# Gather with the one-hot stationary, expert order by a rank product, 22 instead of 25 units in the last layer

## The chip, the cores and the metric

The kernel runs on one core of a Trainium2 chip. The metric is the time of one execution in device microseconds. Three runs of the kernel before took 2532.23, 2533.88 and 2536.08 us; the median is 2533.88.

## The reference

Two layers of a transformer over 256 context tokens and 256 latent tokens with 1024 channels, all in float32. Each layer has a normalisation and one input projection, four groups of heads (gated delta rule, latent attention, windowed attention, dense attention), an output projection and a residual; the change touches none of that. Then comes a mixture of experts, which is the part that the change is in:

```python
scores = sigmoid(h @ router_w)                      # tokens x 64 experts
_, idx = top_k(scores + router_bias, 6)
gates = take(scores, idx); gates = gates / sum(gates) * 2.5
# for each token: sum over its 6 experts of
#   gate * ((silu(h @ gate_w[e]) * (h @ up_w[e])) @ down_w[e])
routed + swiglu(h, shared_gu, shared_down)
```

Each expert has 1024 x 768 gate and up weights and 384 x 1024 down weights. The first layer routes 512 tokens, the last layer only the 256 latent ones, since only these are the output.

## The kernel before

The mixture of experts is worked in units of 128 rows (slots). A unit takes the tokens of one to four experts, in groups of 32 slots: one expert with all four groups, one with three groups and another with one, two experts with two groups each, or four experts with one group each (a quad). Experts are sorted by how many tokens chose them (`cnt`, `key`, `rank`), and the rank decides the kind of unit. In the last layer there are 25 units: 4 of one expert, 4 of 3 + 1 groups, 8 pairs, 9 quads; `last_work` (L658) puts their order down, a quad, then a unit of one or (3 + 1) kind and a pair, and so on. Two units of the shared expert (n = 0 and 1) come before all of them. `EARLY` is 2, the number of the first routed unit.

Weights come in tiles of [128 x 3072] words (1536 KB), three for each expert: `lo` and `hi` (the lower and upper half of the contraction of gate and up) and `down`. SyncE's queue loads them in the order in which TensorE uses them, lo(n), hi(n), down(n-1), into a ring of nine tiles (`ring`, L721): a load is issued when the part that used the tile before has been multiplied. The loads' experts are read from `eid`; the first layer waits twice for it, for its first eight entries and then (`sorted_ready`, L1021) for all 64. The ninth load waits for that in the first layer.

For each unit n of the last layer, TensorE does in this order (L1769 to L1783): the lo part, the transposes of the activations of n-1 (`act_transposed`), the gate rows of n-1 (`gate_rows`), the hi part, the first pair of combining products of n-2 (`combine`), the gather of n+1 (`gather_by_product`, L1704), the second pair, and the down product of n-1. `gather_by_product` makes the transposed rows of the unit's tokens at once: for each of eight slices of channels and two tiles of tokens it multiplies the tokens (stationary, 128 columns) with a one-hot matrix `hot` of token and slot (128 columns moving), and VectorE copies the result to `hgT` (`unit_copied`, L2601). VectorE also multiplies silu by up (`unit_times`), makes the one-hots (`one_hot`), adds the combined rows (`added`) and copies half of each unit's result (`unit_out`); ScalarE computes silu, copies transposed activations and the other half. The first layer gathers by an indirect DMA of GpSimd and then transposes on TensorE (`unit_transposed`, L1642).

Before the units stands the routing, mostly a chain on VectorE (L2732 to L2817), where each step waits for the one before (`link`): scores plus bias, the eight largest and their indices for each tile of tokens, one-hot over chosen experts, their sum `mask`; TensorE sums the mask to positions and counts (`positions`, L1543); then the sort key, ranks, and in the first layer the lists of tokens by unit. There the order `eid` comes from eight rounds of maximum, index and replacement (`sorted_round`, L2763), the first before the ranks and seven after the lists. In the last layer it comes from a one-hot by rank and a product (`order_of_experts`, L1559).

Of the kernel before, what the change touches and what calls it, by code (L numbers as in the profile page):

```python
# [13 lines left out]
P = 128  # L14
# [23 lines left out]
NT = 4  # L38
# [29 lines left out]
for _n, _w in (("ident", P), ("inc_f", P), ("inc_b", P), ("str_f", P), ("str_b", P), ("ones", P), ("eye64", HALF),  # L68
               ("blocks_f", 3 * HALF), ("blocks_b", 3 * HALF), ("window", 2 * SEQ), ("cos_hd", 2 * 6 * HD),
               ("sin_hd", 2 * 6 * HD), ("cos_pe", 2 * HEADS * MLA_ROPE), ("sin_pe", 2 * HEADS * MLA_ROPE),  # L70
               ("experts", NE), ("slot_no", P), ("codes", NT * CODES)):
# [5 lines left out]
LAST_CAPS = ((4, 4), (4, 3), (16, 2), (40, 1))  # L77


def last_columns():  # L80

    whole = [[(u, i) for i in range(4)] for u in range(4)]
    big = [[(u, 0), (u, 1), (u, 2), (67 - u, 0)] for u in range(4, 8)]
    pair = [[(r, 0), (r, 1), (r + 1, 0), (r + 1, 1)] for r in range(8, 24, 2)]
    quad = [[(r + i, 0) for i in range(4)] for r in range(24, 60, 4)]
    return whole + big + pair + quad
# [10 lines left out]
for _n, _w in (("col_rank", N_COL), ("col_from", N_COL), ("marked", P), ("slot_of", 4), ("index", 1)):  # L97
    TABLE[_n] = (_at, _at + _w)
    _at += _w
# [15 lines left out]
def constants():  # L115
# [30 lines left out]
    put("slot_no", np.arange(P)[None, :])  # L146
    token = np.arange(P)[:, None, None] + P * np.arange(NT)[None, :, None]
# [11 lines left out]
    row("index", p[:, None])  # L159
# [46 lines left out]
def build(nc, x, c, ctx, c_ctx, w_mod, b_mod, norm1_g, norm2_g, rows, taps, w_in, w_up, w_out, router_w,  # L206
          exp_w_gu, exp_w_down, shared_w_gu, shared_w_down, consts, out):
    with ExitStack() as stack:
# [190 lines left out]
        cnt, key, rank, base, cap, left = (scratch(NE) for _ in range(6))  # L399
        gate = sb("gate", [P, NT, 8])  # L400
        beats = carve(stat, 224, NE)
        unit_hot = carve(stat, 288, NE)
        row64 = carve(stat, 352, NE)
# [37 lines left out]
        gated = [carve(htreg, 3072, 2 * P), carve(htreg, 3584, 2 * P)]  # L441
# [192 lines left out]
        order_psum = Order("order_psum", ("router", "pos", "rank", "list"),  # L634
                           ("router", "pos", "marks", "eid", "places", "shares", "rank"))
        order_made = Order("order_made", ("mask", "beats", "listT"), ("mask", "perm", "beats", "shares", "rank"))
# [12 lines left out]
        gate_psum = sig("gate_psum", [N_LAST])  # L649
        gated_ready = sig("gated_ready", [N_LAST])  # L650
# [7 lines left out]
        def last_work():  # L658

            units = {kind: [u for u in range(N_LAST) if KIND_OF[u] == kind] for kind in range(4)}  # L660
            order = []
            for i, quad in enumerate(units[3]):
                order.append(quad)
                if i < 4:
                    order += [units[0][i], units[2][i]]
                elif i < 8:
                    order += [units[1][i - 4], units[2][i]]
# [68 lines left out]
        slotT_psum = sig("slotT_psum", NQ)  # L736
# [350 lines left out]
        def _(pe):  # L1087
# [83 lines left out]
            for l in LAYERS:  # L1171
# [386 lines left out]

                def order_of_experts():  # L1559
# [197 lines left out]
                if l == LAST:  # L1757
# [11 lines left out]
                    for n in range(EARLY, NW[l] + 1):  # L1769
# [11 lines left out]
                        if n >= EARLY + 2:  # L1781
                            combine(n - 2, 1)
# [1286 lines left out]
```

## Time and profile before

| | |
|---|---|
| profiled execution | 2537.54 us, span 2535.7 us, mean granted TensorE clock 0.969 |
| TensorE (PE) busy | 2305.1 us, 91% of the span |
| VectorE (DVE) busy | 792.5 us, 31% |
| ScalarE (ACT) busy | 403.7 us, 16% |
| GpSimd (POOL) busy | 229.0 us, 9% |
| expert loads | 256 + 128 of 1536 KB each, both layers |
| costliest line | L1675 (lo and hi parts), 749.0 us busy, 119.0 us idle before |
| gather by product, L1715 | 191.5 us busy, 800 records |

Line numbers are those of the kernel before. A busy matmul is an occupied one, not one at peak; a share of DMA is the mean of 16 engines. PEld is the load of the stationary operand, which runs beside the products. One float32 product shows as two records.

### The profile page before, as it was taken

How to read it: one execution, taken by the hardware profiler on the slowest of the kernel's cores; microseconds unless marked ns; L12 is line 12 of the kernel's file. 1: busy time of each engine (PE TensorE's matmuls, PEld its weight loads, DVE VectorE, ACT ScalarE, POOL GpSimd, SP SyncE). 2: the span in 40 equal slices, each digit the busy share in tenths (PEclk: the TensorE clock that was granted, in tenths of full speed). 3: DMA queues.
4: the chain of work that ended last, by engine and by line, in shares of the span. 5: the costliest groups of instructions: out<-in, count | busy, mean ns of one | idle time of the engine just before them, and what ended most of it. 6: DMA issues, size and time to landing. Idle time of an engine off the chain costs nothing. (4 is left out here: it accounts for less than half of the span.)

```text
span 2535.7 us, 40724 instructions
## 1 busy us (share of the span) xinstructions
PE 2305.1 (91%) x17170; PEld 1241.6 (49%) x17170; DVE 792.5 (31%) x1709; ACT 403.7 (16%) x860; POOL 229.0 (9%) x286
## 2 busy tenths in 40 slices
PE   6999899999877888888897998899999999999998
PEld 2456744454333343334343556755655565555553
DVE  2375745262110101111112546753222222212123
ACT  2323344110000000000001233352000000000000
POOL 0007200011101111110001005300000000000000
PEclk9999999999999999999998999999999999999999
DMA  8000197359999999999997310015999999999997
GB/s 333 34 17 36 65 379 305 135 226 413 427 426 417 417 419 417 417 419 399 385 422 303 129 50 21 28 47 212 404 390 377 376 423 367 429 412 424 408 416 297
DMA packets 86042, 762.18 MB, mean 301 GB/s; under 512 B 14376, under 2 KB 14904, under 8 KB 27232
## 3 DMA queue, kind: packets, MB, share of 16 engines
q1 hardware_dynamic: 74720, 734.30, 70.3%
q0 software_dynamic: 11136, 25.20, 2.6%
q8 instruction: 141, 2.31, 0.3%
q14 instruction: 45, 0.37, 0.0%
HBM read 748.54 MB, written 23.49 MB: 304 GB/s over the span
## 5 line engine op out<-in xcount | busy, mean ns | idle before, releaser
L1675 PE MATMUL banks<-arena,htreg 128*32 128x384 f32 (+2 forms) x5312 | 749.0, 521 | 119.0 <-DMA arena<-in_exp_w_gu 113.8
L1675 PEld LDWEIGHTS banks<-arena,htreg 128*32 128x32 f32 (+2 forms) x5312 | 331.7, 132 | 527.4 <-issue 435.1
L1700 PE MATMUL banks<-arena,modreg 128*32 128x512 f32 (+2 forms) x1992 | 351.6, 597 | 20.4 <-issue 19.1
L2556 DVE TENSOR_TENSOR modreg<-modreg,banks 128x384 f32<-128x384 f32 x65 | 36.0, 554 | 687.1 <-ACT modreg L2056 687.1
L1700 PEld LDWEIGHTS banks<-arena,modreg 128*32 128x32 f32 (+2 forms) x1992 | 117.4, 126 | 222.1 <-issue 220.7
L1715 PEld LDWEIGHTS banks<-htreg,hreg 128*128 128x128 f32 x800 | 194.2, 334 | 8.7 <-issue 5.9
L1715 PE MATMUL banks<-htreg,hreg 128*128 128x128 f32 x800 | 191.5, 398 | 0.0
L1196 PE MATMUL banks<-arena,htreg 128*128 128x512 f32 (+3 forms) x480 | 158.9, 490 | 0.0
L2079 ACT ACTIVATE modreg<-banks 128x512 f32<-128x512 f32 x58 | 34.7, 598 | 589.5 <-PE banks L1700 589.5
L2617 DVE COPY modreg<-banks 128x512 f32<-128x512 f32 x58 | 40.1, 692 | 268.5 <-PE banks L1700 268.5
L1196 PEld LDWEIGHTS banks<-arena,htreg 128*128 128x128 f32 x480 | 89.6, 191 | 65.0 <-issue 61.0
L1742 PE MATMUL banks<-modreg,htreg 128*128 128x512 f32 x200 | 98.0, 614 | 3.1 <-issue 2.0
L2056 ACT ACTIVATE modreg<-banks 128x384 f32<-128x384 f32 x65 | 31.9, 491 | 432.0 <-PE banks L1675 432.0
L2062 ACT ACTIVATE modreg<-banks 128x384 f32<-128x384 f32 x65 | 31.9, 491 | 422.8 <-PE banks L1691 422.8
L2604 DVE COPY htreg<-banks 128x512 f32<-128x512 f32 x61 | 42.2, 691 | 170.4 <-PE banks L1715 167.6
L1515 PE MATMUL banks<-arena,htreg 128*128 128x512 f32 x192 | 83.2, 593 | 0.0
L2972 POOL DMA_INDIRECT htreg<-h_d,lsg x34 | 35.1, 1032 | 514.5 <-PE banks L1653 472.8
L1184 PE MATMUL banks<-htreg,arena 128*128 128x512 f32 (+1 forms) x192 | 76.1, 558 | 1.2 <-ACTq L780 0.8
L1470 PE MATMUL banks<-arena 64*128 64x512 f32 (+3 forms) x144 | 71.6, 579 | 2.5 <-ACT arena L1990 2.5
L2663 DVE TENSOR_TENSOR hreg<-hreg,banks 128x512 f32<-128x512 f32 x96 | 63.8, 684 | 6.9 <-PE banks L1742 5.9
L1289 PE MATMUL banks<-arena 64*64 64x64 f32 x1280 | 52.8, 224 | 10.7 <-DVE arena L2476 4.0
L1515 PEld LDWEIGHTS banks<-arena,htreg 128*128 128x128 f32 x192 | 36.2, 190 | 44.1 <-issue 44.0
(439 smaller groups left out, 2235.3 us busy)
## 6 DMA issues: line engine op xcount, KB each, us to landing
arena<-in_exp_w_gu SPq DMA_DIRECT2D x256, 1536.0 KB, 17.3
arena<-in_exp_w_down SPq DMA_DIRECT2D x128, 1536.0 KB, 21.5
arena<-in_w_mod SPq DMA_DIRECT2D x32, 1024.0 KB, 9.9
modreg<-in_w_mod SPq DMA_DIRECT2D x14, 1024.0 KB, 8.0
arena<-y_d SPq DMA_DIRECT2D x4, 3072.0 KB, 17.8
modreg<-mod_d SPq DMA_DIRECT2D x20, 512.0 KB
arena<-in_shared_w_gu SPq DMA_DIRECT2D x6, 1536.0 KB
arena<-in_w_in SPq DMA_DIRECT2D x4, 2048.0 KB, 12.7
```

Source lines behind the costliest of these rows:

```text
L1184: last = mm(qkv_bank(ct)[:, lo:], win_qkv[:, k, tok(ct)], hT[:, k, lo:], start=(i == 0), stop=(i == KD - 1))
L1196: last = mm(ps[2 + n % 4][:, lo:w], hT[:, k, tok(t)], win[g][:, k, lo:w], start=(k == 0), stop=(k == KD - 1))
L1289: last = mm(out[r, at + HALF * g:at + HALF * g + HALF], lhs(r, g), rhs(r, g), start=True, stop=True)
L1470: mm(ps[s % 2][:, 0:nk * P], q_, k_, start=True, stop=True).then_inc(scores_psum.sem, 1)
L1515: last = mm(ps[2 + n % 2][:], mixT[:, k, tok(t)], wout[:, k, 512 * half:512 * half + 512], start=(k == 0), stop=(k == KD - 1))
L1675: last = mm(gu_bank(n, half)[rows, 0:DE], src[:, k, rows], up4[q][:, i, DE * half:DE * (half + 1)], start=(k == 0), stop=(k == KD - 1))
L1700: last = mm(ps[4 + half][rows, :], actT[:, k, rows], dn3[q][:, k, 512 * half:512 * half + 512], start=(k == 0), stop=(k == KE - 1))
L1715: last = mm(ps[k // 4][:, tok(k % 4)], rows[:, k, :], hot[r % 2][:, j, :], start=(j == 0), stop=(j == 1))
L1742: mm(comb_bank(n, j, half), gated[r % 2][:, P * j:P * j + P], outs[r % 2][:, 512 * half:512 * half + 512], start=True, stop=True).then_inc ...
L2604: dve.tensor_copy(hgT[q % 2][:, 0:4, :], ps[0][:].rearrange("p (k n) -> p k n", k=4))
L2617: dve.tensor_copy(outs[r % 2][:, 512:1024], ps[5][:]).then_inc(unit_y.sem, 1)
L2663: tt(acc_last[:, j, cols], acc_last[:, j, cols], gu_bank(n + 1, half)[:], ALU.add).then_inc(comb_added.sem, 1)
```

## The change

In the last layer the gather is turned round: the one-hot is stationary and the tokens move, 512 columns at a time, so four products give the unit's rows [128 slots x 1024]. ScalarE copies them to `hrow` in two halves, TensorE transposes them in eight pieces (`rows_transposed`, behind the second pair of combining products), and VectorE copies these to `hgT` as before, now behind both pairs of additions. The capacities change: no unit of one expert is left; 4 units of 3 + 1 groups, 8 pairs and 10 quads make 22, and the order becomes quad, one or two others, quad. In both layers the mask is made by comparing the scores with a copy in which the six largest have been replaced; indices and one-hots come later (first layer: right behind the mask; last layer: behind the first unit's copy). In the first layer the sort rounds 2 to 8 are replaced by a one-hot by rank, a product with the column 0 to 63 (`index`, moved to the other table of constants) and a copy; and the position products move ahead of the lo part of unit 1.

```diff
-LAST_CAPS = ((4, 4), (4, 3), (16, 2), (40, 1))
+LAST_CAPS = ((4, 3), (16, 2), (44, 1))
-    whole = [[(u, i) for i in range(4)] for u in range(4)]
-    big = [[(u, 0), (u, 1), (u, 2), (67 - u, 0)] for u in range(4, 8)]
-    pair = [[(r, 0), (r, 1), (r + 1, 0), (r + 1, 1)] for r in range(8, 24, 2)]
-    quad = [[(r + i, 0) for i in range(4)] for r in range(24, 60, 4)]
+    big = [[(u, 0), (u, 1), (u, 2), (63 - u, 0)] for u in range(4)]
+    pair = [[(r, 0), (r, 1), (r + 1, 0), (r + 1, 1)] for r in range(4, 20, 2)]
+    quad = [[(r + i, 0) for i in range(4)] for r in range(20, 60, 4)]
...
+            others = [u for two in zip(others[4:8] + others[0:2], others[8:12] + others[2:4]) for u in two]
-            for i, quad in enumerate(units[3]):
+            for i, quad in enumerate(quads):
                 order.append(quad)
+                gaps = len(quads) - 1
+                order += others[len(others) * i // gaps:len(others) * (i + 1) // gaps]
...
+                def experts_by_rank():
+                    pe.wait_ge(order_made.sem, order_made.after(l, "perm"))
+                    mm(ps[1][0:1, 384:384 + NE], K("index")[0:NE], by_rank, start=True, stop=True).then_inc(order_psum.sem, 1)
...
+                    for half in range(2):
+                        cols = slice(512 * half, 512 * half + 512)
+                        for j in range(2):
+                            last = mm(ps[half], hot[r % 2][:, j, :], h[:, 2 + j, cols], start=(j == 0), stop=(j == 1))
+                        last.then_inc(slotT_psum.sem, 1)
+                def rows_transposed(n):
+                    r = n - EARLY
+                    pe.wait_ge(slot_rows.sem, slot_rows.at(0, 2 * r + 2))
+                    src = hrow.rearrange("p (d k) -> p k d", k=KD)
                     for k in range(KD):
-                        for j in range(2):
-                            rows = h[:, 2 + j, :].rearrange("p (d k) -> p k d", k=KD)
-                            last = mm(ps[k // 4][:, tok(k % 4)], rows[:, k, :], hot[r % 2][:, j, :], start=(j == 0), stop=(j == 1))
+                        last = pe.transpose(ps[k // 4][:, tok(k % 4)], src[:, k, :], ident)
                     last.then_inc(slotT_psum.sem, 1)
...
                         if n >= EARLY + 2:
                             combine(n - 2, 1)
+                        if n + 1 < NW[l]:
+                            rows_transposed(n + 1)
                         unit_down(n - 1)
...
+                    positions()
                     unit_part(1, "lo")
-                    positions()
                     act_transposed(0)
                     ranks()
+                    experts_by_rank()
...
+                    def slot_rows_copied(n):
+                        r = n - EARLY
+                        for half in range(2):
+                            act.wait_ge(slotT_psum.sem, slotT_psum.at(LAST, 3 * r + half + 1))
+                            fn(hrow[:, 512 * half:512 * half + 512], ps[half][:], ACT.Copy).then_inc(slot_rows.sem, 1)
...
                             added(n - 2, 0)
+                            added(n - 2, 1)
                         if n + 1 < NW[l]:
                             unit_copied(n + 1)
-                        if n >= EARLY + 2:
-                            added(n - 2, 1)
...
-                    link(dve.max_index(out=idx8[:, i, :], in_max=top8[:, i, :], in_values=selb[:, i, :]))
-                link(dve.tensor_copy(idxf[:, nt_, :], idx8[:, nt_, :]))
+                link(dve.tensor_copy(top6[:, nt_, 0:TOPK], top8[:, nt_, 0:TOPK]))
                 for i in range(n_t):
-                    link(tt(onehot[:, i], bc(K("experts"), 1, TOPK), bc(idxf[:, i, 0:TOPK], 2, NE), ALU.is_equal))
-                    ins = red(mask[:, i, :], onehot[:, i].rearrange("p k e -> p e k"), AX, ALU.add)
...
+                    link(dve.match_replace(out=adr[:, i, :], in_to_replace=top6[:, i, :], in_values=selb[:, i, :], imm_value=-3e38))
+                tt(mask[:, nt_, :], selb[:, nt_, :], adr[:, nt_, :], ALU.not_equal).then_inc(order_made.sem, 1)
...
+                ts(by_rank, K("experts")[lo64], rankcol[lo64], None, ALU.is_equal).then_inc(order_made.sem, 1)
...
+                dve.wait_ge(order_psum.sem, order_psum.after(l, "eid"))
+                dve.tensor_copy(eid[0:1, 8:NE], ps[1][0:1, 392:384 + NE]).then_inc(sorted_ready.sem, 1)
...
-                for j in range(1, NE // 8):
-                    sorted_round(j)
```

## Rows read from the trace of the kernel before

**Rows 1.** Stretches of time: stretch, us, busy us (instructions) by engine, clock, DMA share, GB/s.
```profile
1850.00:2140.00 290.00, 290.00 (x1603) 165.15 (x1600) 65.06 (x113) 16.30 (x31) 0.00 (x0) 1.00 0.94 390
2140.00:2450.00 310.00, 300.03 (x2014) 162.51 (x2014) 64.65 (x113) 15.81 (x30) 0.00 (x0) 0.97 1.00 420
2150.00:2200.00 50.00, 50.00 (x341) 25.92 (x338) 10.20 (x18) 3.16 (x6) 0.00 (x0) 1.00 1.01 429
...
556.00:562.00 6.00, 4.91 (x16) 2.32 (x14) 3.08 (x15) 0.60 (x1) 0.30 (x1) 0.90 0.56 165
640.00:1190.00 550.00, 447.41 (x3059) 203.80 (x3052) 59.36 (x95) 36.95 (x70) 67.25 (x67) 0.93 1.01 419
```

**Rows 2.** The same view, two stretches of 10 us in the last layer.
```profile
1920.00:1930.00 10.00, 10.00 (x75) 3.29 (x75) 2.71 (x5) 0.60 (x1) 0.00 (x0) 1.00 0.40 139
...
2220.00:2230.00 10.00, 8.14 (x66) 3.13 (x67) 0.00 (x0) 0.49 (x1) 0.00 (x0) 0.68 1.01 429
```

**Rows 3.** Waits in the last layer: who waited for whom, us, times, longest.
```profile
PE banks L1675 <- DMA arena<-in_exp_w_gu: 15.6, 5, 4.4
...
SPq L1009 <- PE banks L1700: 341.0, 24, 15.4
```

**Rows 4.** Expert loads: issues and size, time to landing, first issues of the last layer.
```profile
arena<-in_exp_w_gu SPq DMA_DIRECT2D x256, 1536.0 KB, 17.3
...
DMA to landing us min/median/max: 6.2/14.3/20.2
...
1763.05 31.21 SPq L1009 DMA_DIRECT2D arena<-in_exp_w_gu  x10
```

**Rows 5.** Timeline of TensorE, one unit: start us, us, line, operation, shapes [idle before].
```profile
2082.01 7.65 PE L1715 MATMUL banks<-htreg,hreg 128*128 128x128 f32 x32
...
2091.31 5.36 PE L1700 MATMUL banks<-arena,modreg 128*32 128x512 f32 x48
2096.60 5.38 PE L1675 MATMUL banks<-arena,htreg 128*64 128x384 f32 x32
...
2108.76 1.98 PE L1742 MATMUL banks<-modreg,htreg 128*128 128x512 f32 x4
2110.58 7.65 PE L1715 MATMUL banks<-htreg,hreg 128*128 128x128 f32 x32
```

**Rows 6.** Timeline of TensorE, eight transposes of a unit in the first layer.
```profile
572.79 1.05 PE L1653 MATMUL banks<-const,htreg 128*128 128x128 f32 x8
```

**Rows 7.** Timeline of ScalarE and VectorE in the last layer.
```profile
1840.99 0.60 ACT L2079 ACTIVATE modreg<-banks 128x512 f32<-128x512 f32 x1 [12.31 <-PE banks L1700]
...
1803.98 0.56 DVE L2556 TENSOR_TENSOR modreg<-modreg,banks 128x384 f32<-128x384 f32 x1 [14.16 <-ACT modreg L2056]
```

**Rows 8.** Timeline of TensorE, the last layer's position products.
```profile
1756.27 0.51 PE L1546 MATMUL banks<-arena,const 128*128 128x192 f32 x2
```

**Rows 9.** Timeline of TensorE at the end: last hi part, last down.
```profile
2493.99 8.03 PE L1675 MATMUL banks<-arena,htreg 128*32 128x384 f32 x64 [3.02 <-DMA arena<-in_exp_w_gu]
...
2518.62 5.36 PE L1700 MATMUL banks<-arena,modreg 128*32 128x512 f32 x48
```

**Rows 10.** Timeline of VectorE, first layer: mask's ends, and parts of a sort round.
```profile
520.31 0.42 DVE L2735 TENSOR_TENSOR arena<-arena,small 128x256 f32<-128x256 f32 x1 [5.19 <-ACT arena L2036]
...
528.28 0.81 DVE L2742 TENSOR_REDUCE arena<-modreg 128x64 f32<-128x384 f32 x1
...
552.29 0.22 DVE L2764 MAX8 arena<-arena 128x8 f32<-128x64 f32 x1
...
552.96 0.21 DVE L2772 MATCH_REPLACE8 arena<-arena 128x64 f32<-128x64 f32 x1
```

**Rows 11.** Timeline of the load queue, first layer's first expert loads.
```profile
534.65 3.25 SPq L1009 DMA_DIRECT2D arena<-in_exp_w_gu  x4
...
559.64 1.95 SPq L1009 DMA_DIRECT2D arena<-in_exp_w_gu  x4
```

**Rows 12.** Timeline of TensorE, first layer's rank product.
```profile
533.19 0.43 PE L1575 MATMUL banks<-stat,const 64*128 64x64 f32 x2 [1.45 <-DVE stat L2760]
```

More of the change, by code:

```diff
@@ L70 @@
                ("sin_hd", 2 * 6 * HD), ("cos_pe", 2 * HEADS * MLA_ROPE), ("sin_pe", 2 * HEADS * MLA_ROPE),
-               ("experts", NE), ("slot_no", P), ("codes", NT * CODES)):
+               ("experts", NE), ("slot_no", P), ("codes", NT * CODES), ("index", 1)):
     CONST[_n] = (_at, _at + _w)
@@ L96 @@
 _at = 0
-for _n, _w in (("col_rank", N_COL), ("col_from", N_COL), ("marked", P), ("slot_of", 4), ("index", 1)):
+for _n, _w in (("col_rank", N_COL), ("col_from", N_COL), ("marked", P), ("slot_of", 4)):
     TABLE[_n] = (_at, _at + _w)
@@ L146, in constants @@
     put("slot_no", np.arange(P)[None, :])
+    put("index", np.arange(P)[:, None])
     token = np.arange(P)[:, None, None] + P * np.arange(NT)[None, :, None]
@@ L398, in build @@
         gatesum, cntmax, next8 = scratch(NT), scratch(8), scratch(8)
-        cnt, key, rank, base, cap, left = (scratch(NE) for _ in range(6))
+        cnt, key, rank, base, cap = (scratch(NE) for _ in range(5))
+        top6 = scratch(NT, 8)
         gate = sb("gate", [P, NT, 8])
@@ L402, in build @@
         unit_hot = carve(stat, 288, NE)
+        by_rank = carve(modreg, 2048 + DE + 1024, NE, part=NE)
         row64 = carve(stat, 352, NE)
@@ L440, in build @@
         hot = [carve(htreg, 2048 + 512 * b, 2, P) for b in range(2)]
-        gated = [carve(htreg, 3072, 2 * P), carve(htreg, 3584, 2 * P)]
+        gated = [carve(htreg, 2304 + 512 * b, 2 * P) for b in range(2)]
+        hrow = carve(htreg, 3072, D)
         acc_last = carve(hreg, 0, 2, D)
@@ L658, in last_work @@
         def last_work():
-            units = {kind: [u for u in range(N_LAST) if KIND_OF[u] == kind] for kind in range(4)}
+            quads = [u for u in range(N_LAST) if KIND_OF[u] == 3]
+            others = [u for u in range(N_LAST) if KIND_OF[u] != 3]
+            others = [u for two in zip(others[4:8] + others[0:2], others[8:12] + others[2:4]) for u in two]
             order = []
-            for i, quad in enumerate(units[3]):
+            for i, quad in enumerate(quads):
                 order.append(quad)
[L664 to L667, printed above, removed]
+                gaps = len(quads) - 1
+                order += others[len(others) * i // gaps:len(others) * (i + 1) // gaps]
             return [(u, tuple(dict.fromkeys(r for r, _ in COLUMNS[u]))) for u in order]
```

49 lines of the change are left out of this document (24 added, 25 removed).

## The prediction

> **What bounds the kernel now.** I read the stretches of time first. The last layer's experts fill 1763 to 2536 us, and two engines work at their limit there in turn: from 1850 to 2140 TensorE is busy all 290 us while the DMA share is 0.94; from 2140 to 2450 the share is 1.00 and TensorE stands for 10 us; in 2150 to 2200 the DMAs move 429 GB/s at a share of 1.01 [rows 1]. The share falls behind a unit with one expert (128\*128 form): 0.40 in 1920 to 1930, one of four such dips [rows 2], since such a unit asks for three weight tiles in one TensorE period and then all nine tiles are full. The waits say the same: TensorE waits for weights 15.6 us in all here, the load queue waits for TensorE's down products alone 341 us [rows 3]. In the first layer, from 640 to 1190, the share is 1.01 and TensorE is busy 447 of 550 us [rows 1]. So the first layer goes at the pace of the loads, and the last one at TensorE's, with the loads close behind.
>
> **The floor that the loads set.** The diff moves no weight: 64 experts x 3 loads = 192 in the last layer, before and after, each 1536 KB (1.573 MB) [rows 4]. At 429 GB/s one takes 3.67 us. The shortest issue-to-landing is 6.2 us [rows 4], so 2.5 us lie around a lone load.
>
> **The change in the last layer.** A TensorE period there is now 28.5 us (gather at 2082.01, the next at 2110.58 [rows 5]): down 5.3, lo 5.3, hi 5.3 (it has lo's form), gather 7.5, two pairs of combining products 1.8 each, and 1.5 for a transpose and gate rows.
> - Gather: the 16 products with 128 columns (32 records, 7.5 us) become 4 products with 512 columns (8 records) and 8 transposes. Eight records of 512 columns cost twice the x4 piece of rows 5, 2 x 1.8 = 3.6 us. The eight transposes are the first layer's piece, 1.05 us [rows 6]. 4.6 instead of 7.5 us: 2.9 saved per unit.
> - Units: 25 become 22 (four of one expert go, one of four experts comes). 25 x 28.5 = 713 us become 22 x 25.6 = 563 us.
> - Between products and transposes stands ScalarE's copy of two half rows; a 512-column copy there takes 0.60 us [rows 7], and 0.6 us after the last product is covered by the second combining pair (1.8 us), queued ahead of the transposes. 44 copies are 26 us on an engine that is busy 8 in 50. I take zero; uncovered it is 0.6 x 22 = 13 us of TensorE, still far below the loads. VectorE's second pair of additions now stands before its copy of the transposed rows; 1.4 us, and `down` (5.3 us) covers that copy. The same value, zero; uncovered 1.4 x 22 = 31 us.
> - The one-hot over chosen experts moves behind the first copy in the last layer: about 2 us of VectorE in an idle time of 14.2 us [rows 7]. Zero; 2 us otherwise.
> - The faster mask starts the last layer's loads no earlier. The position products, which need the mask, start at 1756.27 right behind the shared expert's hi part, with no idle time in front [rows 8]: they do not wait for the mask now. So the first load stays at 1763.05 [rows 4].
>
> 563 us of TensorE against 192 x 3.67 = 704 us of loads: the loads become the limit, and the saving of 150 us is mostly given to waiting. Does the ring of nine tiles keep them going? When TensorE waits for the last of four tiles of a part, three are landed and up to five follow behind that one; they are 18 us of loading, and the four tiles come free after 5.4 to 8.0 us [rows 5, 9]. No unit is left that needs fewer than two experts (six loads, 22 us, against 25.6 us of TensorE), and every one or two of these is followed by a quad (44 us of loads). So I expect no dip as in [rows 2].
>
> The end: six `down` loads (two of the last pair, four of the last quad) are ordered behind the last hi load, so this lands at 1763.05 + 2.5 + 186 x 3.67 = 2447.5. From the same point the kernel before took 2535.7 - 2494.0 = 41.7 us [rows 9]; the six loads (22 us) land within the 24.6 us before the last down at 2518.6 [rows 9]. End 2489.2, or 46.5 earlier. But 429 is the best stretch; at 427 GB/s, to leave something for mixed windows, 186 loads take 3 us more. **Term: -43.5 us**; bounds -46.5 (429) and, at the 420 GB/s of 2140 to 2450 and 419 of 640 to 1190 [rows 1], 3.75 us a load, -31.5.
>
> A rule against this sum: the Trainium skill, "DMA: Bandwidth & Descriptors", Specifications, gives an HBM limit of about 358 GB/s per core and a fabric ceiling of 435. By the first the layer would need an estimated 844 us of loads, which the trace excludes (429 GB/s are moved); by the second, 694 us, an estimated end 9 us earlier than my floor, which no stretch here shows.
>
> **The change in the first layer.** The old mask ran on VectorE from the end of the addition at 520.77 to the last reduction's, 528.28 + 0.81 = 529.09 [rows 10]. The new one has four maxima (0.26 each with the gap), a copy (0.2, an estimate below the 0.42 of a width of 256), four match-and-replace (0.34 with their value load) and a comparison (0.42, as wide as the addition) [rows 10]: ready at about 523.8. Then four index searches, cast and one-hots, 4 x 0.34 + 0.2 + 4 x 0.59 = 3.9 us, to 527.7, and `unit_times` to 528.2; the position products, moved ahead of the lo part, are done by 524.4 + 1.8 = 526.2. So VectorE takes positions at 528.2 instead of 531.4, and the first load goes out at 531.4 instead of 534.65 [rows 11]: 3.2 us.
> The seven later sort rounds (from 552.29 [rows 10] on, with the next load at 559.64 [rows 11]) are replaced by one product and a copy (0.4 and 0.2 us), with VectorE waiting about 0.4 us for it; so the order is whole at about 533.5. Before, the sixth load had to wait for it until 559.64, and in 556 to 562 only 165 GB/s moved [rows 1, 11]: 6 us at 0.6 lost plus the edges, about 4 us. Now two more loads leave at once, the next when hi of unit 1 is done.
> TensorE itself gains little: it stood 1.45 us before the rank product [rows 12], pays 0.4 for the new one and its wait, and its lists start about 0.7 us sooner. Until 640 it runs unhindered, so the loads can lead only as far as tiles are free. From 562 to 600 they had some 4 us of backlog: the nine issues up to 592 against 30 us at about 410 GB/s. I take -3.5 us; bounds -0.7 (TensorE's shift) and -7.2 (start and gap in full). After 640 the loads set the pace, and what is gained there stays until the layer's end.
>
> **Sum.** -43.5 - 3.5 = -47. The profiled execution took 2537.54 us (span 2535.7, 1.84 around it), so it would take 2490.5. The runs shown have a median of 2533.88, 3.7 below it; the changed kernel then lies at **2487 us**. Bounds of the terms: -53.7 gives 2480, -32.2 gives 2502.
>
> **Rivals.**
> - The ring starves the loads in groups of four, as it does now between 1850 and 2140. For it: the share is 0.94 there [rows 1]. Against it: those dips follow one-expert units. Its price: 704 / 0.94 = 749, 45 us above my floor, end about 2532; half of that, 2509. Chance 0.12, mostly near the half.
> - Slower than before: TensorE's clock. After a wait of 3.0 us the next part takes 8.03 instead of 5.37 us, and the granted clock in 2220 to 2230 is 0.68 of 2.4 GHz [rows 2, 9], so part of it at 1.2 GHz. The changed kernel waits once or twice in each quad, some 19 times. At 2.7 us each that is 51 us over 22 units: 25.6 becomes 27.9, below the 32.0 us that loads need per unit (704 / 22). It decides only from 32 us on; to reach 2535 it needs 34 us a unit, a third of all work at half clock. At half clock for half the time, 38 us a unit, the end would be at about 2620. Against it: 640 to 1190, which waits constantly, has a granted clock of 0.93 [rows 1]. Chance 0.03. The Trainium skill, "TensorE: Matmul & The Clock Gate", HAM oscillation, warns of this form, DMA waits between bursts that each start cold; the trace agrees that it happens (8.03 us), and the mean of 0.93 says how rarely.
> - The copies cost: slot rows and additions uncovered, 13 + 31 us: 563 becomes 607 us, still below 704; the time stays 2487. It matters only with the clock case and is counted there.
> - The loads are no bound and TensorE's 150 us come out in full: 2384. A share of 1.01 at 429 GB/s speaks against it. Chance 0.01. That the units or the gather don't change as said: 0.01, about 2530.
>
> **Chances.** Forecast 0.83, starving 0.12, clock 0.03, the last two 0.02. The range 2478 to 2506 holds the forecast's bounds and the milder half of the starving. A change of 0.2% (5 us) is about what a measurement of this kernel can tell from none. Faster 0.95, within 0.2% 0.02, slower 0.03.
>
> **What would show it.** Right: from 1770 to 2465 a share of 1.00 or more in every stretch with 425 to 430 GB/s, no stretch under 0.9; TensorE waiting for in_exp_w_gu some 110 to 140 us there instead of 15.6; a gather of 8 records (3.6 us) and 8 transposes (1.05 us) without idle time in front; first loads at about 531 and 1763 us less the first layer's gain; a second-order queue that no longer stands until 559; tail of 42 us behind the last hi load. Wrong: transposes waiting for ScalarE, dips under 0.7 of the DMA share behind pairs, a granted clock below 0.85 over the layer, or the loads of the first layer at the old distance from its end.

## The result, and the profile after

| | before | after |
|---|---|---|
| median of the runs (range, number), us | 2534.98 (2532.23 to 2537.92, 4) | 2513.53 (2511.37 to 2515.67, 4) |
| profiled execution, us | 2537.54 | 2515.67 |
| mean granted TensorE clock | 0.969 | 0.941 |

The ratio is 0.9912, with a 95% interval of 0.9898 to 0.9926: 22 us faster, where 47 were forecast. The time lies 26.5 us above the forecast and 7.5 us above the upper end of its range. The page of the kernel after begins so (busy us, share of the span, instructions):

```profile
span 2513.8 us, 39653 instructions
PE 2183.7 (87%) x16667; PEld 1083.4 (43%) x16667; DVE 769.0 (31%) x1654; ACT 425.1 (17%) x895; POOL 228.7 (9%) x286
```

**The last layer does what was said of it.** One unit there on TensorE's timeline, as the 28.5 us of [rows 5]:

```profile
1895.67 5.38 PE L1682 MATMUL banks<-arena,htreg 128*64 128x384 f32 x32
1900.98 1.99 PE L1757 MATMUL banks<-modreg,htreg 128*128 128x512 f32 x4
1902.80 3.60 PE L1722 MATMUL banks<-hreg,htreg 128*128 128x512 f32 x8
1906.23 1.88 PE L1757 MATMUL banks<-modreg,htreg 128*128 128x512 f32 x4
1907.95 1.05 PE L1730 MATMUL banks<-const,htreg 128*128 128x128 f32 x8
1908.93 5.36 PE L1707 MATMUL banks<-arena,modreg 128*32 128x512 f32 x48
...
1919.59 7.69 PE L1682 MATMUL banks<-arena,htreg 128*32 128x384 f32 x64 [5.31 <-DMA arena<-in_exp_w_gu]
```

The gather is 3.60 us and the eight transposes behind the second combining pair (L1757) are 1.05 us, with no idle time in front: ScalarE's copies are hidden here. TensorE waits for them three times, 0.69 us each: at the layer's first gather and at the next two, where no pair of combining products stands in between yet. The first of them:

```profile
1793.54 1.16 PE L1730 MATMUL banks<-const,htreg 128*128 128x128 f32 x8 [0.69 <-ACT htreg L2114]
```

The unit above then waits 5.31 us for a weight tile. The waits of 1740 to 2520 (total us, times, longest) and the stretch 1800 to 2470 (columns as in [rows 1]) say the same of the whole layer:

```profile
PE banks L1682 <- DMA arena<-in_exp_w_gu: 107.5, 20, 7.9
SPq L1012 <- PE banks L1707: 237.7, 21, 12.2
```
```profile
1800.00:2470.00 670.00, 563.17 (x3698) 226.25 (x3690) 136.16 (x240) 58.74 (x106) 0.00 (x0) 0.90 1.01 424
```

TensorE's wait for weights went from 15.6 us [rows 3] to 107.5, and the DMA share is 1.01 over all 670 us, where 1850 to 2140 had 0.94 [rows 1]. The layer is bound by its loads. Only the rate differs from the 429 GB/s of [rows 1]: 424.

**Where the time went.** Three landmarks divide it. The first load of the last layer goes out at 1775.07 instead of 1763.05 [rows 4], here in the load queue's timeline:

```profile
1775.07 14.85 SPq L1012 DMA_DIRECT2D arena<-in_exp_w_gu  x8
```

So everything ahead of it is 12.0 us longer in these two profiled executions, where 3.5 less were forecast. From there to the end of the span it is 2513.8 - 1775.07 = 738.7 us instead of 2535.7 - 1763.05 = 772.6: 33.9 us won, where 43.5 were forecast. The tail behind the last hi load has its forecast length, 2513.8 - 2472.05 = 41.8 us:

```profile
2472.05 7.93 PE L1682 MATMUL banks<-arena,htreg 128*32 128x384 f32 x64 [6.68 <-DMA arena<-in_exp_w_gu]
...
2496.59 5.36 PE L1707 MATMUL banks<-arena,modreg 128*32 128x512 f32 x48
```

**The first layer.** The loads do start earlier, as [rows 11] were read, and the queue no longer stands until 559.64:

```profile
532.31 2.52 SPq L1012 DMA_DIRECT2D arena<-in_exp_w_gu  x4
535.01 0.33 SPq L1012 DMA_DIRECT2D arena<-in_exp_w_down  x1
536.67 22.67 SPq L1012 DMA_DIRECT2D arena<-in_exp_w_gu  x4
575.23 0.33 SPq L1012 DMA_DIRECT2D arena<-in_exp_w_down  x1
580.40 19.71 SPq L1012 DMA_DIRECT2D arena<-in_exp_w_gu  x4
```

(Loads are counted here as expert loads. What the section on the kernel before calls the ninth load of the first layer, the one that waits for `sorted_ready`, has three tiles of the shared expert ahead of it and is the sixth expert load.) But the tenth load goes out at 575.23, while in the kernel before, where the sixth to the ninth followed only from 559.64 on [rows 11], it went at 567.96:

```profile
567.96 0.33 SPq L1009 DMA_DIRECT2D arena<-in_exp_w_down  x1
```

The tenth load takes the tile that the first routed unit's lo part frees. What holds it stands in GpSimd's and TensorE's timelines of the kernel after:

```profile
553.70 1.03 POOL L2995 DMA_INDIRECT htreg<-h_d,lsg  x1 [24.14 <-DVE lsg L2836]
```
```profile
553.45 5.39 PE L1707 MATMUL banks<-arena,modreg 128*128 128x512 f32 x12 [0.67 <-ACT modreg L2081]
...
563.36 1.97 PE L1660 MATMUL banks<-const,htreg 128*128 128x128 f32 x8 [4.52 <-DMA htreg<-h_d,lsg]
...
566.71 13.51 PE L1682 MATMUL banks<-arena,htreg 128*128 128x384 f32 x32 [1.38 <-DVE htreg L2634]
```

and of the kernel before, at the same place:

```profile
553.21 1.03 POOL L2972 DMA_INDIRECT htreg<-h_d,lsg  x1 [25.53 <-DVE lsg L2811]
```
```profile
559.87 1.04 PE L1653 MATMUL banks<-const,htreg 128*128 128x128 f32 x8
...
562.36 10.59 PE L1675 MATMUL banks<-arena,htreg 128*128 128x384 f32 x32 [1.45 <-DVE htreg L2605]
```

The transposes of the first routed unit (x8) need the rows that GpSimd's indirect DMA gathers. Before, they did not wait for them at all. Now they wait 4.52 us for that DMA, run 1.97 instead of 1.04 us, and the lo and hi parts behind them take 13.51 instead of 10.59 us. The slower parts are the clock: behind the wait its granted share is 0.50, the level of 1.2 GHz, until about 572, where the kernel before had 1.00.

```profile
566.00:568.00 2.00, 1.29 (x2) 0.84 (x3) 1.97 (x5) 0.00 (x0) 0.99 (x1) 0.50 0.99 414
```

So of the 7.3 us that the tenth load is late, 3.5 are the later start of the transposes and 3.9 the lower clock behind it (0.9 in the transposes, 2.9 in lo and hi). Two stretches of the DMA engines, the first of after and the second of before, show what stands in the gather's way and what follows from it:

```profile
556.00:562.00 6.00, 2.84 (x7) 0.95 (x5) 0.00 (x0) 0.60 (x1) 0.04 (x1) 1.00 1.00 419
570.00:577.00 7.00, 7.00 (x19) 3.99 (x18) 2.28 (x7) 0.00 (x0) 0.00 (x0) 0.81 0.24 77
```
```profile
570.00:577.00 7.00, 5.46 (x23) 3.51 (x22) 3.25 (x9) 0.49 (x1) 0.99 (x1) 1.00 1.02 420
```

In 556 to 562 the engines now move 419 GB/s, where before only 165 moved [rows 1]. Those 165 were in good part the gathers themselves. The DMA queues (packets, MB, share of the 16 engines; q0 is GpSimd's, q1 the load queue's) in 556 to 559, first before, where q0 moved alone, then after:

```profile
q0 software_dynamic: 227, 0.64, 63.7%
```
```profile
q1 hardware_dynamic: 109, 1.14, 89.5%
q0 software_dynamic: 32, 0.13, 10.6%
```

The small gather shares the engines with the weights and gets 0.13 instead of 0.64 MB through. TensorE falls back, its tiles come free late, and in 570 to 577 the loads have nothing to fill: 77 GB/s instead of 420. The gap in the loads was not closed but moved, and it came out larger: 348 GB/s in 530 to 640, against 377 before.

### The profile page after: what moved, and what is told of

It is laid out like the page before. It is cut to its first block and busy times, and to the rows that moved or that the text cites. A ratio compares the mean times of both kernels' runs of the same rounds, so it can differ in the third digit from the quotient of the medians.

```text
span 2513.8 us, 39653 instructions
## 1 busy us (share of the span) xinstructions
PE 2183.7 (87%) x16667; PEld 1083.4 (43%) x16667; DVE 769.0 (31%) x1654; ACT 425.1 (17%) x895; POOL 228.7 (9%) x286
## 5 line engine op out<-in xcount | busy, mean ns | idle before, releaser
L1682 PEld LDWEIGHTS banks<-arena,htreg 128*32 128x32 f32 (+2 forms) x5312 | 323.8, 135 | 632.4 <-issue 552.5
L1707 PE MATMUL banks<-arena,modreg 128*32 128x512 f32 (+2 forms) x1992 | 334.0, 597 | 13.8 <-issue 12.3
L1707 PEld LDWEIGHTS banks<-arena,modreg 128*32 128x32 f32 (+2 forms) x1992 | 107.0, 123 | 196.2 <-issue 191.6
L1757 PE MATMUL banks<-modreg,htreg 128*128 128x512 f32 x176 | 86.7, 617 | 3.1 <-issue 2.0
L2692 DVE TENSOR_TENSOR hreg<-hreg,banks 128x512 f32<-128x512 f32 x84 | 57.7, 688 | 78.5 <-PE banks L1757 77.7
L1722 PE MATMUL banks<-hreg,htreg 128*128 128x512 f32 x176 | 79.3, 593 | 0.0
L2680 DVE TENSOR_SCALAR htreg<-banks,xs 128x256 f32<-128x256 f32 x22 | 10.6, 484 | 176.5 <-PE banks L1739 176.5
L1292 PE MATMUL banks<-arena 64*64 64x64 f32 x1280 | 52.7, 224 | 10.7 <-DVE arena L2505 4.0
L1187 PEld LDWEIGHTS banks<-htreg,arena 128*128 128x128 f32 x192 | 36.9, 193 | 42.7 <-issue 37.9
```

The source lines that it names most:

```text
L1187: last = mm(qkv_bank(ct)[:, lo:], win_qkv[:, k, tok(ct)], hT[:, k, lo:], start=(i == 0), stop=(i == KD - 1))
L1292: last = mm(out[r, at + HALF * g:at + HALF * g + HALF], lhs(r, g), rhs(r, g), start=True, stop=True)
L1682: last = mm(gu_bank(n, half)[rows, 0:DE], src[:, k, rows], up4[q][:, i, DE * half:DE * (half + 1)], start=(k == 0), stop=(k == KD - 1))
L1707: last = mm(ps[4 + half][rows, :], actT[:, k, rows], dn3[q][:, k, 512 * half:512 * half + 512], start=(k == 0), stop=(k == KE - 1))
L1722: last = mm(ps[half], hot[r % 2][:, j, :], h[:, 2 + j, cols], start=(j == 0), stop=(j == 1))
L1757: mm(comb_bank(n, j, half), gated[r % 2][:, P * j:P * j + P], outs[r % 2][:, 512 * half:512 * half + 512], start=True, stop=True).then_inc ...
```

## The experiments

Each median has its range and number of runs; ratios are to the kernel before, run on the same chip. "First load" is the first load of the last layer, read from the profile: 1763.05 before, 1775.07 after.

**Split by layer: e2 and e3.** e2 is the kernel before with the last layer's part alone: gather, units, order.

> The kernel before with the last layer's part alone: gather with the one-hot stationary, 22 units, the new order of units. Mask, sort rounds and the place of the position products stay as before. Theory A (the first layer's part costs time: its early loads stand in the DMA queues when the first two units' rows are gathered): the first layer is as before, the last layer's first load goes out at about 1763 us and the last layer takes 34 us less, as in the changed kernel: 2535 - 34 = 2501 us. Theory B (the 12 us that the changed kernel is late at the last layer's first load have nothing to do with the first layer's part, but with a slower DMA stretch or the run): 2510 to 2514, late again by about 10 us at the last layer's start.

Measured: 2494.61 us (2494.20 to 2497.76, 5 runs), 0.9841 [0.9828, 0.9854]: 40 us faster, and 6 us below what was expected by theory A. First load at 1764.98. So the last layer's part gives alone what had been forecast for it within 3 us, and the rest of the change takes 19 us away. In 2160 to 2210 this kernel loads at 428 GB/s:

```profile
2160.00:2210.00 50.00, 50.00 (x267) 20.63 (x268) 12.50 (x22) 5.54 (x10) 0.00 (x0) 1.00 1.01 428
```

e3 is the kernel after with the last layer's gather and 25 units of before. It keeps the first layer's part and the column of `index`, of which more below.

> The changed kernel with the last layer's gather, its 25 units and their order put back: the mask by comparison, the order by a rank product and the position products moved ahead are left. Theory A: slower than before, TensorE stands some 4 us before the first unit's transposes at about 560 us, that unit's lo and hi take 13.5 instead of 10.6 us, the DMA engines run dry near 572, and the first layer ends 7 to 11 us late: 2542 to 2546 us. Theory B: 2532 to 2536.

Measured: 2547.23 us (2541.86 to 2549.53, 6 runs), 1.0043 [1.0030, 1.0056]: 12 us slower by the medians, 8 to 14 by the interval. First load at 1772.82, and the same wait as in the kernel after:

```profile
563.13 1.73 PE L1659 MATMUL banks<-const,htreg 128*128 128x128 f32 x8 [3.18 <-DMA htreg<-h_d,lsg]
...
566.25 12.61 PE L1681 MATMUL banks<-arena,htreg 128*128 128x384 f32 x32 [1.38 <-DVE htreg L2612]
```

The two differences, -40 and +12, make -28; the whole change gives -22. The loss is in what e3 keeps. That it costs 6 us more in the whole change, where the loads are the limit to the end, is explained by the place of the weight tiles (below), which e3 moves as well and e2 does not.

**The queue in front of the gathers: e1.** The load queue waits, before the sixth load, until both gathers have landed:

```diff
                             sp.wait_ge(sorted_ready.sem, sorted_ready.at(l, 2))
+                            for b in range(2):
+                                sp.wait_ge(gathered[b].sem, gathered[b].at(l, 1))
```

> The changed kernel, where in the first layer the loads from the third routed unit on (the sixth load of experts and later) wait until the gathered rows of the first two units have landed. Theory A: the gathers find an almost empty queue as before, land within about 5 us, TensorE transposes without a wait at about 560 us and the queue doesn't run dry at 572; the loads lose some 3 us at 552 to 558 and win back more: first layer 6 to 9 us shorter than in the changed kernel, 2503 to 2507 us. Theory B: a wait more can only delay loads; 2513 to 2518.

Measured: 2506.83 us (2505.05 to 2508.62, 4 runs), 0.9888 [0.9874, 0.9902]: 7 us below the kernel after, though its load queue issues nothing from 533.9 to 560.2:

```profile
533.58 0.34 SPq L1012 DMA_DIRECT2D arena<-in_exp_w_down  x1
560.16 2.39 SPq L1012 DMA_DIRECT2D arena<-in_exp_w_gu  x4
```

First load at 1766.86, 8.2 us earlier than in the kernel after. The gather's rows are there when TensorE comes, earlier even than before:

```profile
557.22 1.05 PE L1662 MATMUL banks<-const,htreg 128*128 128x128 f32 x8
```

The first two gathers land 4.8 us after their issue (median), where the kernel after needs 11.4. A theory of the loads alone can't give this, since e1 issues them later; the queue in front of the gathers is shown. But the time was still 20 us above the forecast, and in 1800 to 2470 the rate still 424 GB/s. That pointed to a second cause.

**The place of the weight tiles: e6, e6b, e9.** The column of `index` makes the table `const` one column wider. Buffers are laid out one behind the other in steps of 32 bytes, so the buffer `arena`, in which the tiles lie, moves from a multiple of 256 bytes to 32 bytes behind one. e6 puts `const` behind it and the small `convw` in front of it, which brings `arena` back to a multiple of 256 bytes. The buffers behind `const` stay off one, so it is the place of `arena` that is tried:

```diff
+        A_WORDS = 30720
+        convw = sb("convw", [P, 6, CONV])
+        arena = sb("arena", [P, A_WORDS])
         const = sb("const", [P, N_CONST])
-        A_WORDS = 30720
-        arena = sb("arena", [P, A_WORDS])
...
-        convw = sb("convw", [P, 6, CONV])
```

> The changed kernel with its buffers laid out in another order, so that the region that all weight tiles lie in starts at a multiple of 256 bytes in a partition, as in the kernel before (the one column more of the constants had put it 32 bytes behind one). Nothing else. Theory C (the shifted destination costs the loads 1%: 424 against 429 GB/s in the last layer, 417 against 419 to 421 in the first): 427 to 429 GB/s between 1800 and 2470 us, 8 us less in the last layer and 4 to 6 in the first, 2500 to 2504 us. Theory D (the slower stretches come from the deeper queue or from the order of the work, not from the place): 424 GB/s as before, 2511 to 2516 us.

Measured: 2501.34 us (2493.71 to 2503.31, 4 runs), 0.9860 [0.9843, 0.9876]: 12 us below the kernel after. e6b leaves the order and adds 32 bytes more between them (`pad = sb("pad", [P, 8])`), so that `arena` is 64 bytes behind a multiple of 256.

> The changed kernel with 32 bytes between the constants and the region of the weight tiles, which then starts 64 bytes behind a multiple of 256. If only 64 bytes matter: as with the full 256, 2500 to 2504 us. If a start off a multiple of 256 costs whatever its distance: 424 GB/s and 2511 to 2516 us. Theory D: 2511 to 2516 us.

Measured: 2509.73 us (2508.00 to 2512.05, 4 runs), 0.9899 [0.9885, 0.9913], 1.3 us below what was expected if any distance costs. Two stretches where the loads are the limit, first of e6, then of e6b:

```profile
640.00:740.00 100.00, 80.28 (x796) 33.91 (x792) 10.11 (x16) 6.31 (x12) 12.02 (x12) 0.93 1.01 427
2160.00:2210.00 50.00, 49.71 (x269) 21.17 (x268) 13.05 (x22) 5.23 (x10) 0.00 (x0) 1.00 1.01 429
```
```profile
640.00:740.00 100.00, 79.70 (x784) 33.58 (x780) 10.10 (x16) 6.32 (x12) 12.06 (x12) 0.93 1.01 424
2160.00:2210.00 50.00, 50.00 (x284) 20.68 (x278) 12.27 (x21) 5.55 (x10) 0.00 (x0) 0.98 1.01 424
```

Tiles at multiples of 256 bytes load at 427 and 429 GB/s, tiles 64 bytes off at 424 in both. e9 is the kernel before with the same 32-byte pad.

> The kernel before with 32 bytes put between the constants and the region of the weight tiles, so that this starts 32 bytes behind a multiple of 256. Theory C: the loads fall to 423 to 425 GB/s in 640 to 740 and 2150 to 2200 us; 4 to 6 us in the first layer, and 2 to 4 in the last, where TensorE is mostly the limit: 2541 to 2545 us. Theory D: no change, 2533 to 2537 us.

Measured: 2538.38 us (2535.83 to 2546.93, 8 runs), 1.0023 [1.0012, 1.0035]: 3.6 us slower. Its rates, with the columns as above:

```profile
640.00:740.00 100.00, 79.41 (x774) 33.14 (x777) 11.63 (x19) 6.32 (x12) 13.10 (x13) 0.93 1.01 423
2160.00:2210.00 50.00, 50.00 (x319) 27.98 (x315) 11.65 (x20) 2.16 (x5) 0.00 (x0) 1.00 1.01 424
```

The rate falls as said, from 427 and 429 to 423 and 424, by an edit that touches nothing but addresses. The time is less clear. Five of its eight executions took 2535.8 to 2538.9 us and three 2544.3 to 2546.9, so the median lies under the expectation of 2541 to 2545, while the ratio's interval of 0.12% to 0.35% is 3 to 9 us. The profiled execution was the shortest of the eight; where it lost and won is in the table of landmarks below.

The Trainium skill, "DMA: Bandwidth & Descriptors", How a descriptor splits into AXI transactions, says that a descriptor which does not start at a multiple of 256 bytes begins with a transaction from the boundary below, whose bytes ahead of the start are fetched unused and still cost time. The direction agrees with the 424 against 429 GB/s. But the page speaks of bytes fetched, and here the source stayed where it was and the destination moved; that this rule is the reason no run here shows.

**Both mended: e10, and its wait one load later: e11.** e10 has e1's wait and e6's layout.

> The changed kernel with both mendings: loads from the third routed unit on wait for the first two gathers, and the weight tiles' region starts at a multiple of 256 bytes. If the queue in front of the gathers and the place of the tiles are the two causes and add up: 2506.8 - 12 = 2493 to 2497 us, no worse than the last layer's part alone (2494.6), and 2 to 3 us better if the earlier first load counts. If the place doesn't matter: 2505 to 2509 us.

Measured: 2492.63 us (2490.95 to 2494.24, 5 runs), 0.9833 [0.9820, 0.9845], at the lower end of what was expected. First load at 1759.80. Its last hi part begins here:

```profile
2448.53 6.81 PE L1684 MATMUL banks<-arena,htreg 128*32 128x384 f32 x64 [7.72 <-DMA arena<-in_exp_w_gu]
```

e11 waits for the gathers at the seventh expert load instead of the sixth (`loaded` counts the three tiles of the shared expert too):

```diff
+                    if l < LAST and loaded == SLOTS:
+                        for b in range(2):
+                            sp.wait_ge(gathered[b].sem, gathered[b].at(l, 1))
```

> As the kernel with both mendings (2492.6 us), but one expert load more goes out before the wait for the two gathers: the sixth load leaves at about 536 us instead of 559.5. Theory A, with the queue's length as the cause: five loads end at about 551, the sixth near 555, two us after the first gather is issued (552.3), so the gather lands 1 to 3 us later and TensorE with it, while the loads have won 3.7 us: 2489 to 2493 us. If any backlog at the gather's issue makes it as slow as in the changed kernel: TensorE waits 3 to 5 us near 558 and starts cold, 2495 to 2500 us.

Measured: 2490.95 us (2486.11 to 2494.01, 5 runs), 0.9817 [0.9804, 0.9830], the lowest median of all, though its interval overlaps that of e10. The transposes wait 0.61 us:

```profile
559.27 1.16 PE L1663 MATMUL banks<-const,htreg 128*128 128x128 f32 x8 [0.61 <-DMA htreg<-h_d,lsg]
```

The four kernels with and without the two mendings are a table that adds up within the intervals: neither 2513.5, wait 2506.8 (-6.7), layout 2501.3 (-12.2), both 2492.6 (-20.9, against a sum of -18.9).

**Where each cause lies.** One more landmark divides the time ahead of the last layer's first load. Right behind the first layer's last expert load the load queue issues the load of `list_d`, here before, after and in e10:

```profile
1325.01 0.43 SPq L1038 DMA_DIRECT2D modreg<-list_d  x1
```
```profile
1335.70 0.43 SPq L1041 DMA_DIRECT2D modreg<-list_d  x1
```
```profile
1324.83 0.43 SPq L1043 DMA_DIRECT2D modreg<-list_d  x1
```

| profiled execution, us | `list_d` | from there to the last layer's first load | from that load to the end |
|---|---|---|---|
| before | 1325.01 | 438.0 | 772.6 |
| e9, before with the tiles moved | 1329.80 | 433.3 | 770.9 |
| e2, last layer's part alone | 1326.91 | 438.1 | 730.9 |
| after | 1335.70 | 439.4 | 738.7 |
| e1, wait | 1329.23 | 437.6 | 738.3 |
| e6, layout | 1330.71 | 438.2 | 730.1 |
| e10, both | 1324.83 | 435.0 | 729.4 |

The first column takes the two causes apart. The place of the tiles costs 4.8, 5.0 and 4.4 us in the first layer (e9 to before, after to e6, e1 to e10), the queue in front of the gathers 6.5 and 5.9 us (after to e1, e6 to e10). In the last layer the place costs 8.6 and 8.9 us where the loads are the limit (after to e6, e1 to e10) and nothing in e9, half of whose last layer goes at TensorE's pace. The middle column differs by up to 6 us between kernels, 4.7 us between before and e9, whose programs are the same there but for addresses, and in e14, whose first layer is that of e10, it is 431.7 instead of 435.0; a gain or loss of a few us at the last layer's first load is therefore not a measure of the first layer's part. That is how e9's first load comes out no later than before.

**What each part of the last layer is worth: e5 and e12.** e5 is the kernel after with the old gather of 16 products.

> The changed kernel with the old gather (16 products of 128 columns on the one-hot, 7.5 us) but 22 units. If the loads are the limit of the last layer (28.5 us of TensorE a unit against 32.4 us that 192 loads at 424 GB/s need per unit): within 3 us of the changed kernel, 2513 to 2517 us, with the waits for weights down from 107 to about 45 us. If the gather carries half of the gain: 22 x 2.9 = 64 us of TensorE, of which at least 10 to 20 come out, 2525 to 2535.

Measured: 2521.05 us (2517.46 to 2526.43, 4 runs), 0.9951 [0.9933, 0.9968]: 7.5 us above the kernel after by the medians, 10 by the ratios, not within 3. Its waits for weights:

```profile
PE banks L1680 <- DMA arena<-in_exp_w_gu: 61.5, 13, 8.6
```

e12 is e10 with the 25 units and the order of before, so the new gather alone.

> The kernel with both mendings, with the old 25 units and their order, gather as changed. TensorE needs 25 x 25.6 = 640 us, the loads 704. If only the sum of either counts: as with 22 units, 2491 to 2495 us. If the units of one expert (three loads in 25.6 us of TensorE) still fill all nine tiles: dips of the DMA share behind them, some 4 to 6 us each four times, 2500 to 2515 us.

Measured: 2500.08 us (2497.43 to 2501.21, 4 runs), 0.9854 [0.9839, 0.9869]: 7.5 us above e10. Its waits, and the stretch 1800 to 2450:

```profile
PE banks L1685 <- DMA arena<-in_exp_w_gu: 52.1, 13, 7.7
```
```profile
1800.00:2450.00 650.00, 610.52 (x3784) 259.61 (x3780) 153.29 (x265) 66.45 (x120) 0.00 (x0) 0.97 1.00 425
```

On TensorE the gather saves 2.9 x 22 = 64 us and the units 610.5 - 553.2 = 57 us, with e10's 553.19 busy in the same stretch. Both together brought 40 us (e2), and each one adds only some 7.5 to the other: with either alone the layer is already close to the loads' pace, and most of what the second saves becomes waiting. Of the four dips that the expectation of e12 names, its DMA share shows one clear one, 0.73 in 1830 to 1840, and the rate over the stretch is 425 against e10's 429; how much of the 7.5 us is that was not tried by itself.

**Is the ring long enough, and are the loads the bound: e13 and e14.** e13 is e10 with eight tiles instead of nine in the last layer.

> The kernel with both mendings, with eight instead of nine weight tiles in the last layer's ring. The argument of the prediction: four tiles are waited for, the others follow in flight, 3.67 us each; with eight tiles four remain, 14.7 us against 5.4 to 8 us until tiles come free: no dip, 2491 to 2496 us. If the ring is near its limit: dips of the DMA share in each quad, 10 x 2 x 1 to 2 us, 2510 to 2530 us.

Measured: 2496.30 us (2495.26 to 2497.92, 4 runs), 0.9844 [0.9829, 0.9859]: 3.7 us more than e10, though the intervals of the ratios overlap.

```profile
1800.00:2450.00 650.00, 553.72 (x3642) 223.10 (x3631) 134.90 (x234) 58.26 (x105) 0.00 (x0) 0.92 1.01 427
```

A share of 1.01 even with a tile less, and 0.96 in its lowest 10 us: no dips behind pairs or quads. With eight tiles the rate is 427 against e10's 429 GB/s. With nine the ring does not starve the loads, since from 1790 to 2470 the kernel after has 1.00 in its lowest 10 us. e14 is e10 with half of each weight load in the last layer, so it leaves half of the weights out:

```diff
+                    if l == LAST:
+                        dst, src = dst[:, 0:CHUNK // 2], src[:, 0:CHUNK // 2]
```

> The kernel with both mendings; each load of the last layer brings only the first half of its tile, so half of each weight tile there keeps older contents: what is left is TensorE's own pace. If the loads are the bound and TensorE's saving was given to waiting: units of 25.6 us without waits for weights, 22 x 25.6 = 563 us between the first unit's start at about 1782 and 2345, the end 27 us later, 2370 to 2380 us. If TensorE or its neighbours (copies, additions, clock) are the bound: near 2490.

Measured: 2373.92 us, one run. Its waits for weights, and the stretch 1800 to 2340:

```profile
PE banks L1686 <- DMA arena<-in_exp_w_gu: 15.3, 6, 3.4
```
```profile
1800.00:2340.00 540.00, 523.98 (x3654) 213.82 (x3651) 134.88 (x235) 56.82 (x103) 0.00 (x0) 0.99 0.70 256
```

With the share at 0.70, TensorE is busy 524 of 540 us and the kernel ends 2492.6 - 2373.9 = 119 us earlier. So the loads are the bound of the last layer, and most of the 150 us that TensorE saved is given to waiting, as the prediction said.

## Why the prediction was wrong, step by step

The miss of 26.5 us is 15.5 us ahead of the last layer's first load (+12.0 for -3.5), 9.6 us behind it (-33.9 for -43.5), and 1.4 us in the step from the profiled execution to the median.

- **The last layer's mechanism: right.** Loads as the limit; 563 us of TensorE (563.17 busy in 1800 to 2470, where that the digits meet is chance: the window cuts both ends and some parts ran at the lower clock); gather 3.6 and transposes 1.05; copies hidden but for three waits of 0.69 us; waits for weights 107.5 us, just under the 110 to 140; tail 41.8 against 41.7 us. e14 shows the bound, and the share of 1.00 in the lowest 10 us of the kernel after shows the ring. One reading was wrong without consequence: ScalarE was taken as busy 8 in 50 us, [rows 1] have 3.16.
- **Its size, "427 GB/s, 3 us more than at 429": the first wrong term.** The rate was 424. The `index` column was known to move to the other table; the prediction asked only what it costs to compute, not what it moves in memory. e6, e6b and e9 show the rate's dependence on the address. With the tiles at a multiple of 256 bytes the last layer takes 730.9, 730.1 and 729.4 us (e2, e6, e10), where 772.6 - 43.5 = 729.1 was forecast. The layout costs the kernel after 12 to 14 us in all, 4.4 to 5.0 in the first layer and 8.6 to 8.9 in the last.
- **"-3.5 for the first layer": the step that failed.** It became +12.0 at the last layer's first load, and +10.7 already at `list_d`: 5 us are the tiles' place, 6 the queue in front of the gathers. The starts came within 1 us of what was worked out (532.31 against 531.4). The gap was read from [rows 1] and [rows 11] as 4 us of lost loading, and its closing was booked as a gain. In that gap the first two gathers went through. The queue that a moved transfer is put in front of was GpSimd's, through the shared DMA engines, and was not asked about. e1 gives 6.7 us back by opening the gap again, and e11 shows that one load more can go out before it at no cost.
- **The gain itself did not come either.** With both causes out, `list_d` is issued at 1324.83 in e10, 1324.77 in e12, 1325.33 in e13, 1325.16 in e14 and 1325.17 in e11, against 1325.01 before and 1326.91 in e2, whose first layer is that of before. So the first layer's part is worth 0 to 2 us there, not 3.5, although the loads start 2 to 4 us earlier. In e11 the tenth load goes out 0.56 us earlier than before, which is the size of the bound "-0.7 (TensorE's shift)"; in e10 3.1 us earlier, and that is lost again by `list_d`. Why is not shown.
- **The bounds.** -0.7 to -7.2 for that layer had no end above zero, so the range could not hold a loss there. The gather had 6.7 us from its issue to TensorE's arrival (553.21 to 559.87) in a stretch at 165 GB/s; a change that fills this stretch with loads needed a bound for its delay, 4.5 us of waiting as it came out, with 3.9 us of the lower clock and more for the tiles freed late behind it.
- **The rivals.** Starving: refuted by the share of 1.01. The clock: granted 0.90 in 1800 to 2470, and quads' parts after waits take longer (7.69 and 7.93 us, against the 5.38 of the pair's part at 1895.67 that did not wait), but TensorE still waited 107.5 us for weights, so it did not decide there. In the first layer a wait did cost clock, 3.9 us behind the first gather, but that came of the gather's delay and the rival had been placed in the last layer. Units and gather unchanged, or no bound by loads: refuted by the rows above and e14. None of the rivals, as priced, was what happened.
- **With both causes out, the total comes near the forecast, in part by luck.** e10's profiled span of 2489.2 with 1.84 around it gives 2491.0 (forecast 2490.5), and its last hi part starts at 2448.53 (forecast 2447.5 + 3 - 3.5 = 2447.0). The last layer's 729.4 us are the forecast's. But the 3.25 us by which e10's first load is earlier than before are 0.2 us up to `list_d` and 3.0 us in the stretch behind it, which varies by that much between kernels that do not differ there. e12, e13 and e14, with the same first layer, have their first loads at 1763.63, 1761.84 and 1756.89. The first layer's term was met there by chance.

What stays open: why the earlier start of the first layer's loads does not last until its end; what in the stretch from `list_d` to the last layer's first load varies by up to 8 us; and by what mechanism the place of the destination costs 1% of the rate. That e10 comes out only 2 us below e2 fits the landmarks: its first layer is 2 us faster at `list_d`.

## What to carry to other kernels

A gap in one queue can be the passage of another: before closing it, list what is issued by any engine in the same stretch, see which queue moved the bytes in it, and when its consumer needs them. When a table of constants grows by a column, see what it pushes: the large DMA destinations behind it may move off a multiple of 256 bytes. And where loads are a few per cent behind TensorE, work out the time at which they take over; what is saved on TensorE after that is waiting. To judge one stage's term, take the landmark at that stage's end: one landmark further on, other stages' variation can look like the forecast coming true.

## What the runs showed of the hardware

- The place of a DMA's destination in the on-chip memory is worth 1% of the load rate: 1536 KB loads moved 429 GB/s at multiples of 256 bytes (e6) and 424 at 32 bytes (the kernel after) or 64 bytes (e6b) behind one, in otherwise equal kernels, and with 32 bytes in 640 to 740 of e9 423 instead of 427.
- A small indirect gather issued while the engines hold queued bulk loads lands late: issued at 553.70, its rows were waited for until 563.36, 9.7 us, where before the issue at 553.21 was followed by TensorE at 559.87 without a wait. The first two gathers landed 11.4 us after their issue in the kernel after and 4.8 us in e1, which holds the loads back (medians).
- A wait of 4.52 us on TensorE was followed by a granted clock of 0.50 for some 8 us: eight transposes took 1.97 instead of 1.04 us, the lo and hi parts behind them 13.51 instead of 10.59 us.
